# A two-layer streaming encoder: the layer and mixing loops written out, the low-rank gate products put behind the first projection tiles, and prologue, layer change and tail rebuilt

## What is computed (the reference, cut)

```python
def layer(x, ...):
    z = rmsnorm(x, norm_mix) @ w_in              # 1024 x 8208
    qa, ka, va, qg, kg, vg, rg, ag, ga, gb = split(z)
    ua = rmsnorm(diff_attend(rope(qa), rope(ka), va), a_subln) @ w_pa
    g  = log_sigmoid(ag @ w_ga2 + b_ga) / 16     # low-rank gate: ag has 16 columns
    og, S = gated_linear_attention(qg, kg, vg, g)
    ub = (rmsnorm(og, g_norm) * silu(rg)) @ w_pb
    x = x + (sigmoid(ga) * ua + sigmoid(gb) * ub) @ w_o
    h = rmsnorm(x, norm_ffn);  x = x + (silu(h @ w_f1) * (h @ w_f3)) @ w_f2
    h = rmsnorm(x, norm_ple);  x = x + sigmoid(h @ w_ple_gate) * (pe @ w_ple)
    return x                                     # and K, V, S as outputs
y = rmsnorm(x, final_norm)                       # after the second layer
```

## Time and profile before

| what | us |
|---|---|
| median of 3 runs (1622.63 to 1629.17) | 1624.71 |
| span of the profiled execution, first to last instruction | 1626.9 |
| PE busy | 1541.7 (95%) |
| DVE busy | 870.3 (53%) |
| ACT busy | 619.2 (38%) |
| POOL busy | 256.6 (16%) |
| first tile of layer 1, of layer 2 (start in the span) | 44.2, 842.9 |
| last matmul of the last tile of layer 1 ends | 809.9 |
| last matmul of the last tile of layer 2 ends, span ends | 1608.6, 1626.9 |

### The profile page before, as it was taken

How to read it: one execution, slowest core, us unless ns; L and a number is a source line. 1 busy time by engine, 2 the same in 40 slices (tenths; PEclk the granted TensorE clock), 3 DMA queues, 4 the chain that set the end, 5 groups by cost and what they waited for, 6 DMA issues and landing times.

```text
span 1626.9 us, 27470 instructions
## 1 busy us (share of the span) xinstructions
PE 1541.7 (95%) x10005; PEld 1428.1 (88%) x10005; DVE 870.3 (53%) x1404; ACT 619.2 (38%) x1028; POOL 256.6 (16%) x295
## 2 busy tenths in 40 slices
PE   3999999999999999999958999999999999999997
PEld 1888888898899999999837898888988999999996
DVE  3554636546366655545445545464555565555554
ACT  2333333434363433333243342433435434333342
POOL 3300203021002200013303020030300040000233
PEclk9988989989899999999969989899998999999998
DMA  4333343355334444544637634355431444445442
GB/s 137 90 100 90 95 124 95 86 105 98 99 104 155 149 140 150 163 143 147 112 50 107 120 86 112 73 114 124 90 90 60 154 155 155 141 144 161 160 141 70
DMA packets 195152, 190.79 MB, mean 117 GB/s; under 512 B 9078, under 2 KB 192188, under 8 KB 195100
## 3 DMA queue, kind: packets, MB, share of 16 engines
q1 hardware_dynamic: 191984, 181.76, 42.3%
q0 software_dynamic: 2688, 7.35, 1.2%
q10 hardware_dynamic: 428, 1.03, 0.2%
HBM read 181.45 MB, written 8.65 MB: 117 GB/s over the span
## 4 chain that ended last, share of the span: by engine, by line
PE 80%; DMA 5%; issue 5%; POOL 4%; DVE 3%; ACT 2%; SPq 0%; DVEq 0%; ACTq 0%; POOLq 0%
PE big L1120 22%; PE big L1121 20%; PE big L1122 20%; DMA w_raw<-in_w_in 5%; PE X L1293 2%; PE X L1258 2%; POOL E L503 2%; PE X L1257 2%; POOL rot L510 1%; PE X L1240 1%; PE X L1209 1%; PE X L1202 1%; POOL E L504 1%; PE X L1130 1%; PE X L1159 1%
## 5 line engine op out<-in xcount | busy, mean ns | idle before, releaser
L1120 PE MATMUL big<-x_hi,w_hi 128*128 128x320 f32 x1984 | 656.2, 331 | 16.5 <-DVE z L869 9.6
L1122 PE MATMUL big<-x_hi,w_lo 128*128 128x320 f32 x1984 | 625.9, 315 | 0.0
L1121 PE MATMUL big<-x_lo,w_hi 128*128 128x320 f32 x1984 | 625.9, 315 | 0.0
L798 DVE TENSOR_TENSOR w_lo<-w_raw,w_hi 128x1024 fp32r<-128x1024 f32 (+1 forms) x330 | 415.1, 1261 | 138.5 <-ACT w_hi L535 138.3
L1120 PEld LDWEIGHTS big<-x_hi,w_hi 128*128 128x128 f32 x1984 | 382.9, 193 | 55.3 <-issue 26.7
L535 ACT CAST w_hi<-w_raw 128x1024 fp32r<-128x1024 f32 x328 | 330.3, 1036 | 157.6 <-PE big L1122 95.3
L1121 PEld LDWEIGHTS big<-x_lo,w_hi 128*128 128x128 f32 x1984 | 385.2, 194 | 3.0 <-issue 1.6
L1122 PEld LDWEIGHTS big<-x_hi,w_lo 128*128 128x128 f32 x1984 | 384.1, 194 | 0.0
L470 POOL TENSOR_TENSOR sqt<-xT 128x320 f32<-128x320 f32 x56 | 57.3, 1022 | 653.6 <-DVE xT L1073 422.8
L1120 PE MATMUL big<-h_hi,w_hi 128*128 128x320 f32 x352 | 108.6, 309 | 0.0
L1122 PE MATMUL big<-h_hi,w_lo 128*128 128x320 f32 x352 | 108.4, 308 | 0.0
(11 more groups left out here) (212 smaller groups left out, 1930.6 us busy)
## 6 DMA issues: line engine op xcount, KB each, us to landing
w_raw<-in_w_in SPq DMA_DIRECT2D x130, 512.0 KB, 7.5
w_raw<-in_w_f SPq DMA_DIRECT2D x120, 512.0 KB, 4.2
w_raw<-in_w_pb SPq DMA_DIRECT2D x16, 512.0 KB, 4.3
w_raw<-in_w_pa SPq DMA_DIRECT2D x16, 512.0 KB, 4.0
w_raw<-in_w_o SPq DMA_DIRECT2D x16, 512.0 KB, 3.9
w_raw<-in_w_ple_gate SPq DMA_DIRECT2D x16, 512.0 KB, 4.5
w_raw<-in_w_f SPq DMA_DIRECT2D x16, 384.0 KB, 3.6
k_raw<-in_cache_k SPq DMA_DIRECT2D x8, 256.0 KB, 8.8
```

The lines of the kernel that those rows point to most:

```text
L798: tt(w_lo[:, t % 4, 0:nk, :], w_raw[:, (t // 2) % 2, 0:nk, (t % 2) * P:(t % 2 + 1) * P], w_hi[:, t % 4, 0:nk, :].bitcast(F32), ALU.subtrac ...
L1120: mm(out, wh, xh[:, k0 + k, :], start=start and k == 0, stop=False)
L1121: mm(out, wh, xl[:, k0 + k, :], start=False, stop=False)
L1122: last = mm(out, wl, xh[:, k0 + k, :], start=False, stop=stop and k == nk - 1)
```

## The change

Python loops over constants take the place of the hardware loops over layers and over mixing iterations on every engine (the loops of merge, FFN up, FFN down on some engines stay). Semaphore values in them become constants. The 16-column gate product moves behind tile 0, the four products with `ga2` behind tile 1, the logs on ACT to t == 2, the decays on DVE to t == 2 of a layer's first iteration, and there ACT's exponentials to t == 6, behind `hi` of tile 8. For the second layer `norm_sums` moves behind tile 0 as well. `w_ag` and `ga2` are loaded behind the first weight unit (first layer) and behind the merge stage (for the second layer). In the prologue the gains are transposed before x, the squares of x come from ACT over token rows with a diagonal product on PE (`dg`), and the lambdas are finished at t == 2, with a matmul behind tile 3. At the end, the gain is applied per chunk in the last PLE tiles (`xf`), transposes follow, token sums come from six small matmuls, and the scale by `rstd_tok` is part of the last copies, with six stores. `mix_hi` and `mix_lo` get space of their own.

The diff, cut to its core and with its indent reduced:

```diff
-with sp.Fori(0, DEPTH) as l:
-    sp.dma_start(w_ag[:, :, :], w_in[:, bass.ds(l * KC, KC), C_AG:C_AG + RANK]).then_inc(ag_in, 16)
-    sp.dma_start(ga2[:, None, :], w_ga2[:, bass.ds(l, 1), :]).then_inc(ag_in, 16)
-    with sp.Fori(0, MIX_IT) as j:
...
+def gate_inputs(l):
...
+    if l:
+        sp.wait_ge(agg_ready, l)
+        sp.wait_ge(g_done, l)
+    sp.dma_start(w_ag[:, :, :], w_in[:, l * KC:(l + 1) * KC, C_AG:C_AG + RANK]).then_inc(ag_in, 16)
...
+    sp.dma_start(ga2[:, None, :], w_ga2[:, l:l + 1, :]).then_inc(ag_in, 16)
+for l in range(DEPTH):
+    for j in range(MIX_IT):
+        tb = snap(sp, l * TILES + j * MIX_N)
         qk_unit(tb, l, j)
+        if l == j == 0:
+            gate_inputs(0)
...
         sp.wait_ge(x_trans, KC)
+        sp.wait_ge(xsq_ready, 3)
...
+    if l < DEPTH - 1:
+        gate_inputs(l + 1)
...
 for t in range(3):
...
-    sp.dma_start(dst, x_tok[0:rows(t), t, :]).then_inc(y_stored, 16)
...
+    for half in (1, 0):
+        sp.wait_ge(y_copied[half], t + 1)
+        c = slice((1 - half) * (D // 2), (2 - half) * (D // 2))
+        dst = y_p[:, t, c] if t < 2 else y_s[:, c]
+        sp.dma_start(dst, x_tok[0:rows(t), t, c]).then_inc(y_stored, 16)
...
-clear_ssq(None)
-for c in range(KC):
-    square((c, c + 1, c < KC - 1), slice(c, c + 1))
...
-    with pool.Fori(0, iters - 1) as j:
-        for t in range(per):
-            n = pool.snap(l * 24 + j * per + (8 * norm + t))
...
+    for c in range(last):
+        square((n0 + c, n0 + c + 1, c < last - 1), slice(c, c + 1))
...
+    squares_of_loop(l, 3, KC if l < DEPTH - 1 else KC - 1)
...
-for t in range(2):
-    act.wait_ge(raw_in[0], 32)
-    nc.scalar.copy(w_hi[:, t, :, :], w_raw[:, 0, :, t * P:(t + 1) * P]).then_inc(hi_ready, 1)
+for half in range(2):
+    act.wait_ge(x_in[half], 32)
+for t in range(3):
...
+    nc.scalar.activation(x_junk[0:rows(t), :], x_tok[0:rows(t), t, :], ACT.Square,
+                         accum_out=xsq[0:rows(t), t:t + 1]).then_inc(xsq_ready, 1)
...
-with act.Fori(0, DEPTH) as l:
-    tables(LN_EXP)
+for l in range(DEPTH):
+    if l:
+        tables(LN_EXP)
...
+        act.wait_ge(x_ready, l * 24 + (m + 1 if l == 0 else KC))
         norm_chunk(l, 0, m, U_MIX)
-    norm_rstd(l, 0)
...
+    if l == 0:
+        norm_rstd(l, 0)
+        for t in range(2):
+            act.wait_ge(raw_in[0], 32)
+            nc.scalar.copy(w_hi[:, t, :, :], w_raw[:, 0, :, t * P:(t + 1) * P]).then_inc(hi_ready, 1)
...
+    def decay_logs():
+        act.wait_ge(zg_ready, l + 1)
+        steps = Steps(act, act_decay, l * 2, 2)
...
+        nc.scalar.activation(lg, lg, ACT.Ln, bias=cst[:, K_ONE:K_ONE + 1]).then_inc(lg_ready, 1)
...
-    with act.Fori(0, MIX_IT) as j:
...
+    for j in range(MIX_IT):
...
-            if t == 3:
+            if j == t == 0 and l:
+                norm_rstd(l, 0)
+            if j == 0 and t == 2:
+                if l == 0:
+                    act.wait_ge(lsum_ready, 1)
+                    nc.scalar.activation(lexp[:, :, :], lsum[:, :, :], ACT.Exp).then_inc(lexp_ready, 1)
+                decay_logs()
+            if t == (6 if j == 0 else 3):
                 act.wait_ge(args_ready, v * (2 * NL + 1))
                 nc.scalar.activation(E[:, 0:NL + 1, :], E[:, 0:NL + 1, :], ACT.Exp).then_inc(decay_ready, 1)
...
 tables(LN_EXP)
-steps = Steps(act, act_rms, 3 * DEPTH, 1)
-rms(rstd[:, :], X[0], 1.0 / D, rstd_ready, steps, norm_sum, 3 * DEPTH + 1)
+act.wait_ge(tok_sums, 1)
 for t in range(3):
...
-    nc.scalar.copy(x_tok[0:rows(t), t, 0:512], X[2 * t][0:rows(t), :]).then_inc(y_copied[1], 1)
+    nc.scalar.activation(rstd_tok[0:rows(t), t:t + 1], X[2][0:rows(t), 2 * t:2 * t + 1], ACT.Ln, scale=1.0 / D,
+                         bias=cst[0:rows(t), K_EPS:K_EPS + 1]).then_inc(tok_logs, 1)
+for t in range(3):
+    act.wait_ge(tok_logs, t + 1)
+    nc.scalar.activation(rstd_tok[0:rows(t), t:t + 1], rstd_tok[0:rows(t), t:t + 1], ACT.Exp, scale=-0.5).then_inc(tok_rstd, 1)
...
+for t in range(3):
+    act.wait_ge(tok_rstd, t + 1)
+    nc.scalar.activation(x_tok[0:rows(t), t, 0:512], X[3 + t][0:rows(t), :], ACT.Copy,
+                         scale=rstd_tok[0:rows(t), t:t + 1]).then_inc(y_copied[1], 1)
...
+def lambdas():
+    dve.wait_ge(lexp_ready, 1)
+    pro.put(tt(lneg[:, :], lexp[:, 1, :], lexp[:, 0, :], ALU.subtract))
...
+    dve.wait_ge(lam_bc, 1)
+    pro.put(nc.vector.tensor_copy(nlam[:, :], X[5][:, 0:DEPTH]))
...
+        pro.put(stt(c5[:, n, :], cst[:, K_B5:K_B5 + 5], nlam[:, n:n + 1], cst[:, K_A5:K_A5 + 5], ALU.mult, ALU.add))
...
-    st.put(stt(c5[:, l, :], cst[:, K_B5:K_B5 + 5], nlam[:, l:l + 1], cst[:, K_A5:K_A5 + 5], ALU.mult, ALU.add))
-st.close()
-for t in range(2):
-    lo(0, t, KC)
...
-    dve.wait_ge(ag_in, l * 32 + 32)
-    tt(w_agg[:, :, :], w_ag[:, :, :], bc(parT[:, bass.ds(l * KC + R_MIX, KC), None], [P, KC, RANK]), ALU.mult).then_inc(agg_ready, 1)
...
+    if l == 0:
+        for m in range(KC):
+            dve.wait_ge(x_trans, m + 1)
+            nc.vector.tensor_copy(xT[:, m, :], X[m % 4][:, 0:T]).then_inc(x_ready, 1)
+        for t in range(3):
+            dve.wait_ge(xsq_ready, t + 1)
+            n = rows(t)
+            ins = nc.vector.tensor_scalar(dg[0:n, t, 0:n], ident[0:n, 0:n], xsq[0:n, t:t + 1], None, ALU.mult)
+        ins.then_inc(dg_ready, 1)
     for m in range(KC):
         lo_chunk(l, 0, m, U_MIX)
...
-    dve.wait_ge(ag_done, l + 1)
-    dve.wait_ge(rstd_ready, l * 3 + 1)
-    tt(agT[:, :], X[1][0:RANK, 0:T], rstd[0:RANK, :], ALU.mult).then_inc(agT_ready, 1)
-    dve.wait_ge(g_done, l + 1)
-    for h in range(GH):
-        ins = nc.vector.tensor_scalar(zg[:, h, :], X[2 + h][:, 0:T], cur[:, U_BG + h:U_BG + h + 1], None, ALU.add)
-    ins.then_inc(zg_ready, 1)
...
+    if l == 0:
+        for t in range(2):
+            lo(0, t, KC)
...
+    dve.wait_ge(ag_in, l * 32 + 32)
+    tt(w_agg[:, :, :], w_ag[:, :, :], bc(parT[:, l * KC + R_MIX:(l + 1) * KC + R_MIX, None], [P, KC, RANK]), ALU.mult).then_inc(agg_ready, 1)
...
+        dve.wait_ge(g_done, l + 1)
+        for h in range(GH):
+            ins = nc.vector.tensor_scalar(zg[:, h, :], X[2 + h][:, 0:T], cur[:, U_BG + h:U_BG + h + 1], None, ALU.add)
...
-    with dve.Fori(0, MIX_IT) as j:
...
+    for j in range(MIX_IT):
...
+        def decays():
+            dve.wait_ge(lg_ready, l + 1)
+            st.put(stt(E[:, NL, :], zg[:, j, :], 0.0, gab[:, j + (2 * KC - GH), :], ALU.min, ALU.subtract))
...
+            nc.vector.tensor_scalar(E[:, NL + 1, :], E[:, NL + 1, :], 1.0 / 16.0, None, ALU.mult).then_inc(bcur_ready, 1)
...
             if t == 0:
+                if j == 0:
+                    dve.wait_ge(rstd_ready, l * 3 + 1)
                 result(0)
                 stt(qg[:, :], big[0][:, 0:T], GDK ** -0.5, rstd[:, :], ALU.mult, ALU.mult).then_inc(result_read, 1)
+                if j == 0:
+                    dve.wait_ge(ag_done, l + 1)
+                    tt(agT[:, :], X[1][0:RANK, 0:T], rstd[0:RANK, :], ALU.mult).then_inc(agT_ready, 1)
...
+                if j == 0:
+                    gates_of_tokens()
+                else:
+                    decays()
             if t == 2:
                 out_tile(z[:, 0, :], t)
+                if l == j == 0:
+                    lambdas()
+                if j == 0:
+                    maps_of(l)
+                    decays()
...
+            if l == DEPTH - 1:
+                dve.wait_ge(x_ready, l * 24 + (24 + m + 1))
+                if m == KC - 1:
+                    tt(last_sq[:, :], x, x, ALU.mult).then_inc(last_sq_ready, 1)
+                nc.vector.tensor_scalar(xf[:, m, :], x, parT[:, R_FIN + m:R_FIN + m + 1], None, ALU.mult).then_inc(y_ready, 1)
...
+dve.wait_ge(y_trans, 2)
 for t in range(3):
-    dve.wait_ge(y_trans, 3 + t + 1)
-    nc.vector.tensor_copy(x_tok[0:rows(t), t, 512:1024], X[2 * t + 1][0:rows(t), :]).then_inc(y_copied[0], 1)
+    dve.wait_ge(tok_rstd, t + 1)
+    nc.vector.tensor_scalar(x_tok[0:rows(t), t, 512:1024], (X[0], big[0], X[1])[t][0:rows(t), :],
+                            rstd_tok[0:rows(t), t:t + 1], None, ALU.mult).then_inc(y_copied[0], 1)
...
-    pe.wait_ge(ssq_ready, count)
+    pe.wait_ge(ssq_ready, count - 1)
...
+pe.wait_ge(par_in, 112)
+nc.tensor.transpose(X[4][:, 0:NPAR], par[:, :], ident[0:NPAR, 0:NPAR]).then_inc(par_trans, 1)
 for m in range(KC):
...
-pe.wait_ge(par_in, 112)
-nc.tensor.transpose(X[4][:, 0:NPAR], par[:, :], ident[0:NPAR, 0:NPAR]).then_inc(par_trans, 1)
-pe.wait_ge(lneg_ready, 1)
-mm(X[5][:, 0:DEPTH], ones[0:1, :], lneg[:, :], start=True, stop=True).then_inc(lam_bc, 1)
-pe.wait_ge(tables_in, 16)
-with pe.Fori(0, DEPTH) as l:
...
+pe.wait_ge(dg_ready, 1)
+pe.wait_ge(x_ready, KC - 3)
+for t in range(3):
+    n = rows(t)
+    last = mm(X[0][:, t * P:t * P + n], ones[0:n, :], dg[0:n, t, 0:n], start=True, stop=True)
+last.then_inc(norm_sum, 1)
...
+    def low_rank():
+        pe.wait_ge(x_ready, l * 24 + 8)
+        pe.wait_ge(agg_ready, l + 1)
+        for k in range(KC):
```

(32 more changed lines are left out.)

228 lines of the change are left out of this document (110 added, 118 removed).

## The result

The changed kernel takes 1571.57 us (median of 4 runs, 1569.18 to 1574.4), the kernel before beside it 1626.94 (1622.63 to 1629.23): ratio 0.9675, 95% interval 0.9641 to 0.971, some 55 us. The forecast was 1593 with a range from 1579 to 1611; the kernel is faster than the lower end. Four more runs of the changed kernel, one of them traced, gave 1571.08.

What follows compares the result with a forecast made beforehand. PE is busy 95% of the span, so only its idle time and slow clock can be won. Terms 8.9 (first layer) + 16.9 (second) + 5.3 (end) = 31.1 us off the median 1624.7 gave 1593; range 1579 to 1611.

Steps and rivals of the forecast that it cites:

- The iterations written out: Mixing iterations: straight code in place of the loop counted as nothing, at most 1.16 x 6 = 7 us to win.
- Its own sign of being wrong: Mixing iterations were to stay 99 us; differing lengths, or PE's first iteration waiting for weights instead of `kr`, would refute it.
- The first layer's term: Entry into layer 1: decays earlier by 6.7 us, plus a 2.15 us wait gone; 8.9 us won (1.7 to 13).
- Second layer: Layer change: 7.2 to the decays, 4.5 from earlier x, 5.2 from late weights; 16.9 us won (7.2 to 21).
- End: After the last update of x: 11.0 us to the end of the span, 5.3 us won (3 to 7).
- Moved at no cost: Output stage, `xf` products, `mix_hi` space, POOL's squares: moved loads and work count nothing; at most a few us if cover goes.
- (a): Entries: weights set the pace, tile 0 five us later, only 14.2 us won, 1610 us; chance 0.17.
- (b): Entries and end: all lower prices hold, 13 + 21 + 7 = 41 us won, 1584 us; chance 0.13.
- (c): Inner loop jumps cost something that idle time hides, 31 + 7 us won, 1586 us; chance 0.04.
- (d): Mixing iterations: fetching straight code stalls PE or DVE, up to 9.89 us each, 1673 us; chance 0.05.
- (e): First iterations: `kr` waits as long as before, decays held back, only the end gains, 1619 us; chance 0.04.

Runs made afterwards that it cites:

- e16: The kernel before, all loops kept, with the score matmuls spread over tiles 10 and 11 and the GLA output matmuls over tiles 14 and 15: 1579.33 us.
- e1: The kernel before with layer and mixing loops written out on all five engines; old prologue, entry order and tail kept: 1580.62 us.
- e10: The changed kernel with iterations 2 to 4 of the mixing stages a hardware loop on PE alone: 1588.80 us.
- e2: The changed kernel with iterations 2 to 4 of each mixing stage put back into a hardware loop on all engines: 1606.18 us.
- e17: The changed kernel with score and GLA output matmuls spread, and four chunks of x transposed ahead of the gains: 1532.10 us.
- e6: The kernel before with only the layer loop written out; mixing loop, order and tail stay: 1610.32 us.
- e18: The kernel before with layer and mixing loops written out on every engine, but the mixing loop kept on PE: 1600.34 us.
- e19: The kernel before with the layer loop written out everywhere, the mixing loop written out on PE alone and kept on the other four engines: 1588.40 us.

## Why the prediction was wrong

The direction and most places were right; the sum came out 23 us short. **The step that failed is "The iterations written out": "So I count nothing here: at most 1.16 x 6 = 7 us to win."** It measured the price of the mixing loop by the idle time that PE shows inside an iteration, and that stayed where it was (1.0 us in five of six, 2.0 in the other). The price was elsewhere, in two places. Its own sign of being wrong, iterations that differ from 99 us, came.

The six later iterations fell from 596.6 to 585.3 us, and e16 shows that hardly any other cost hides in a steady one. Comparing the first iteration with later ones (all looped on PE in that kernel) could not show what the loop did to all of them.

Second, the weights at the entries: the forecast gave the loops no part in when they land; unit 0's landing at 26.39 stood in a bound alone. With PE's loop written out it lands at 16 to 18. The first layer's term has nearly the right size, 8.9 against 10.5, and its steps came as forecast (tile 0 at 24.1 against 23.7, decays at 50.8 against 49.3, `kr` at 60.68 after a wait of 4.5 against 60.4 and 6, `E` at 74.9 against 76). But there were two ways to the same microseconds, and the forecast knew one: the old order without loops reaches `E` at 74.2 (e1), the new order with PE's loop at 76.2 (e10) and with all of them at 80.1 (e2). On top of written-out loops the rework of the prologue and the moved products win nothing there; e17 gets 3 to 4 us by undoing a part of it. The distance from the decays to `kr`, held fixed at 11.15 us, came out at 9.85 and 9.87.

**Second layer**, 16.9 forecast, 23.4 measured. x final after the last PLE product: 8.5 us, before 15.9, so 7.3 won (4.5 taken, up to 9.0 allowed); from x to the decays 26.3 against the forecast 26.5; from there to `E` 23.8 against 32.5, so 8.7 won (5.2 taken). The jump is gone as said. e1 wins 20.0 of the 23.4 by the same rows (791.49 to 853.58 in its trace), so here too the loops did most of it: e6 wins 9.0 with the layer loop alone, e18 11.3, and the rest up to e1 is PE's mixing loop with its late weights. The places that the prediction gave for this layer, 818, 842 and 870, leave out its own 8.9 us from the first.

**End**: 5.3 forecast, with 11.0 us from x final to the end. It took 9.8 (1562.78 to 1572.6), 6.5 less than before. The run without the new tail says 6.4 by the rows and 8 by the medians. Right, toward the upper end of what was allowed.

**Moved at no cost**: held; no wait on PE in the output stage or for `mix_hi` grew.

**The rivals.** (a), weights that set the pace, was wrong in sign: they landed sooner. (b) had no term for the clock and would have been too slow as well. (c) came nearest in kind, with a chance of 0.04 and a price of 7 where the loops inside gave some 30 in the old order; it also looked for idle time. The page behind it, the Trainium skill ("Runtime: NRT & Kernel Launch", Instruction fetch mechanics), advises full unrolling; these runs agree with the advice, but the price that they show lies at the entries and in the clock, and no run shows it at an inner branch (PE idles 1.16 us in a steady iteration with the loops, 1.00 without). (d) did not happen: straight code cost nothing that the traces show. (e) did not happen: `kr` came 6.5 us sooner in the first layer (60.68 against 67.17).

Left open: why PE's loop delays transfers that other engines issue, long before PE enters it (whether it is the loop or the shorter program, or where program and data then lie in memory, was not varied); why the clock falls more often in iterations that are looped on all engines (busy time of six: 589.6, written out 578.3 and 570.9) when neither a shift of 1.8 us nor a small delay does it; and who owns some eleven of the 35 us in e2.

## What to carry to other kernels

A busy engine can still lose time, here 7 of the 99 us of an iteration: multiply PE's busy share by its granted clock in every stage before saying that only idle time can be won. Where matmuls with few columns stand close together, try them spread over more of the dense stream, one set at a time, and look at the whole iteration's clock: here two spreads won 35 us and a third, on top of the first, lost 17, most of it at the full clock. To price a loop, write it out alone and on one engine alone; a loop's cost can stand in another engine's transfers, far from its branch. And take the parts of a change out in more than one order: two of them may win the same time.

## What the runs showed of the hardware that was not expected

In the kernel before (two traces), e6, e16 and e18, all in the old order with the mixing loop on PE, the first weights are cast at 25.1 to 26.6 us; in e1 and e19, with PE written out, at 17.8 and 18.2. The other engines' loops make no such difference (e18 against e19). At the layer change the first unit took 15.2 to 18.7 us to land before and 7.0 to 13.6 after, for the same two transfers of 512 KB.

The granted clock fell while PE was busy throughout: 11.00 of 11.00 us at 0.53 in the stretch at 869. Later mixing iterations of the same matmuls (some 640 rows each, in the orders above) took 91.4, 95.6, 97 and 100 us in written-out kernels and 91.8 and 98.9 in looped ones, with idle time within 0.3 us of each other: the clock alone makes 8.8 us of difference.
